# Two layers of a hybrid backbone on one core: the pieces of the stream work are moved between the engines' programs, and five mixed blocks go ahead of the heads

## The reference, cut to what matters

```
p = p + mu * (0.5 * (left neighbour + right neighbour) - p)
r, k, v, zw, za = split(p)
decay = exp(-exp(-softplus(-(w0 + tanh(zw) @ w2)) - 0.5))      # for each of two directions
a     = sigmoid(a0 + za @ a2)                                    # for each of two directions
kk    = k*k_k / max(norm(k*k_k), 1e-12)
kmod  = k * (1 + (a - 1) * k_a)
```

## Time and profile before

| what | us |
|---|---|
| median of three runs (2557.12 to 2574.31) | 2568.69 |
| the profiled execution's own time | 2581.38 |
| its span | 2579.6 |
| first load of the next stage (the scan) issued | 672.38 |

### The profile page before, as it was taken

The page is one execution under the profiler, slowest core; times in us unless marked ns, Lnnn a source line. Parts: engine busy times, 40 slices in busy tenths (PEclk is TensorE's granted clock), DMA queues, the critical chain, the costliest instruction groups (busy, mean ns, idle before and its releaser), DMA issues. The chain is left out here.

```text
span 2579.6 us, 61157 instructions
## 1 busy us (share of the span) xinstructions
PE 2130.2 (83%) x26174; PEld 1790.7 (69%) x26174; DVE 1292.5 (50%) x2064; ACT 871.7 (34%) x1685; POOL 722.2 (28%) x786
## 2 busy tenths in 40 slices
PE   3899998787367888878599996894999969999988
PEld 1667876565257777777488885673777758888866
DVE  4335467886334444444354443985546524444422
ACT  2223144465234434444133332222334302333311
POOL 2246322211123224233041000343357414100012
PEclk6999998898589999999799997896999979999989
DMA  8556444553322222220321104644344453111162
GB/s 296 180 145 161 131 143 152 180 182 127 112 80 80 64 81 70 61 86 24 87 82 42 42 27 138 189 140 162 105 110 110 112 140 99 58 50 51 39 201 90
DMA packets 228941, 285.70 MB, mean 111 GB/s; under 512 B 61529, under 2 KB 166905, under 8 KB 227649
## 3 DMA queue, kind: packets, MB, share of 16 engines
q1 hardware_dynamic: 190624, 176.52, 22.9%
q0 software_dynamic: 25680, 81.58, 9.9%
q10 hardware_dynamic: 12368, 23.70, 3.1%
HBM read 193.76 MB, written 87.95 MB: 109 GB/s over the span
## 5 line engine op out<-in xcount | busy, mean ns | idle before, releaser
L164 PE MATMUL in_acc<-in_hi,in_whi 128*128 128x512 f32 (+1 forms) x1024 | 400.6, 391 | 19.6 <-DVE in_lo L840 17.6
L164 PE MATMUL in_acc<-in_lo,in_whi 128*128 128x512 f32 (+1 forms) x1024 | 379.6, 371 | 0.0
L164 PE MATMUL in_acc<-in_hi,in_wlo 128*128 128x512 f32 (+1 forms) x1024 | 379.4, 371 | 0.0
L164 PEld LDWEIGHTS in_acc<-in_hi,in_whi 128*128 128x128 f32 x1024 | 199.2, 195 | 72.3 <-issue 42.3
L164 PEld LDWEIGHTS in_acc<-in_lo,in_whi 128*128 128x128 f32 x1024 | 199.2, 195 | 35.2 <-issue 5.3
L164 PEld LDWEIGHTS in_acc<-in_hi,in_wlo 128*128 128x128 f32 x1024 | 198.5, 194 | 33.2
L1939 DVE TENSOR_REDUCE window_top<-window_score 128x1 f32<-128x640 f32 (+1 forms) x128 | 101.3, 791 | 185.2 <-PE window_score L2022 185.1
L1939 DVE TENSOR_REDUCE dense_top<-dense_score 128x1 f32<-128x640 f32 (+1 forms) x144 | 112.3, 780 | 162.0 <-PE dense_score L2026 161.8
L2064 PEld LDWEIGHTS dense_outs<-dense_V,dense_p 128*128 128x128 f32 x1344 | 169.5, 191 | 8.5 <-ACT dense_p L1907 4.9
L2064 PE MATMUL dense_outs<-dense_V,dense_p 128*128 128x65 f32 x1344 | 169.9, 269 | 0.9 <-ACT dense_p L1907 0.8
L2064 PE MATMUL window_outs<-window_V,window_p 128*128 128x65 f32 x1216 | 160.8, 276 | 1.6 <-ACT window_p L1907 1.1
(11 more groups left out here) (268 smaller groups left out, 5161.6 us busy)
## 6 DMA issues: line engine op xcount, KB each, us to landing
streams<-in_streams_out POOLq DMA_DIRECT2D x40, 512.0 KB, 3.8
scan_L<-streams SPq DMA_DIRECT2D x80, 256.0 KB, 3.7
in_wl<-in_w_mod ACTq DMA_DIRECT2D x32, 512.0 KB, 4.5
in_raw<-in_w_in_even SPq DMA_DIRECT2D x28, 512.0 KB, 4.3
in_raw<-in_w_in_odd SPq DMA_DIRECT2D x20, 512.0 KB, 4.0
close_ga<-gates SPq DMA_DIRECT2D x18, 512.0 KB, 4.1
in_wm<-in_w_mod SPq DMA_DIRECT2D x8, 1024.0 KB, 12.3
gates<-in_outs POOLq DMA_DIRECT2D x32, 256.0 KB, 3.7
```

What stands on the lines that cost most here:

```text
L164: last = pe.matmul(out, a(k), b(k), start=(k == 0 and x == 0), stop=(k == n - 1 and x == 2))
```

## The change

All edits are in the first layer's `projected`; the jobs' order is given where it is called.

- The five mixed blocks zw, za, k0, r0 and v0 come first, then key, value and four query jobs (units 15 to 32), nine mixes (33 to 59), and all eight gates (60 to 83).
- Slots are spread evenly over iterations 38 to 87: 63 slots for 49 units. Two slots fall in iterations 41, 45, 49, 53, 57, 61, 64, 68, 72, 76, 80, 84 and 87. CLEAR_AT stays 36, slot 0 moves to iteration 38.
- PE runs its slots **before** `product(i)`. Its slot t has the first lora product of item t+2, the second of item t+1, `squares(t+1)` and the turned values of t-1. The second lora product and the squares have one buffer each.
- ACT's slot t has `exponentials(t-1)`, `rates(t+1)`, `root_keys(t-1)`, `square_keys(t+2)`, `values_out(t-2)`, in this order. DVE's has `unit_keys(t-2)` or `products(t-2)` with the bonus, then `clamp(t)` or `sums(t)`. POOL stores item t-3.
- The falling exponential is written shifted by one place into chunks of 65 with a 1 at the edge (`falls`, one buffer for each direction). One exponential of ACT and DVE's subtraction go; both products read `falls`. The first step of kmod moves from DVE (L979) to ACT.
- `load_z` has two loads less.

```diff
--- before.py
+++ after.py
...
-    CLEAR_AT, N_AT = 36, 40
+    CLEAR_AT, N_AT, FLUSH = 36, 38, 3
     slot_of_unit = [0] * (NU + 5)
     for u in range(NU + 5):
-        slot_of_unit[u] = min(len(items) + 1, max(0, min(u - N_AT, NSG) + max(0, (u - N_AT - NSG) * 27 // 20)))
+        slot_of_unit[u] = max(0, u - N_AT) * (len(items) + FLUSH) // (NU + 4 - N_AT)
...
-        return range(slot_of_unit[i], len(items) + 1 if i == NU + 3 else slot_of_unit[i + 1])
+        return range(slot_of_unit[i], slot_of_unit[i + 1])
...
-            ksq, root, norm = (st.sb(n, [P, 2, SG]) for n in ("ksq", "root", "norm"))
+            ksq, root, khalf, norm = (st.sb(n, [P, 2, SG]) for n in ("ksq", "root", "khalf", "norm"))
...
-            rate, sigs, cum, before = (st.sb(n, [P, 2, SG]) for n in ("rate", "sigs", "cum", "before"))
-            e_to, b_, bon = (st.sb(n, [P, SG]) for n in ("e_to", "b_", "bon"))
-            km = st.sb("km", [P, 2, SG])
+            rate, cum = (st.sb(n, [P, 2, SG]) for n in ("rate", "cum"))
+            sigs = st.sb("sigs", [P, 3, SG])
+            falls = st.sb("falls", [P, 2, SG // CHUNK, CHUNK + 1])
+            b_, bon = (st.sb(n, [P, SG]) for n in ("b_", "bon"))
+            km = st.sb("km", [P, 2, 2, SG])
...
-                    sp.wait_ge(cleared, 3)
+                    sp.wait_ge(cleared, 4)
                     sp.dma_start(tz[:], rkvz[12]).then_inc(z_in, 16)
-                    for d in range(2):
-                        sp.dma_start(za[(1 - d) * HD:(2 - d) * HD], rkvz[13][d * HD:(d + 1) * HD]).then_inc(z_in, 16)
-                        sp.dma_start(a2s[(1 - d) * HD:(2 - d) * HD], a2[d]).then_inc(dc_in, 16)
+                    sp.dma_start(za[:], rkvz[13]).then_inc(z_in, 16)
+                    sp.dma_start(a2s[:], a2.rearrange("d r n -> (d r) n")).then_inc(dc_in, 16)
...
+                        done = unit_of(items.index(("N", b - 1, NSG - 1)) + 2) + 1 if b else 0
...
+                            free = unit_of(items.index(("X", (q - 2) // NSG, (q - 2) % NSG, 1)) + 2) + 1 if q >= 2 else 0
...
-                        act.wait_ge(refined_k, q - 1)
...
-                    act.activation(ksq[:, q % 2], root[:, q % 2], ACT.Square, scale=0.5 ** 0.5).then_inc(halved_k, 1)
+                    act.activation(khalf[:, q % 2], root[:, q % 2], ACT.Square, scale=0.5 ** 0.5).then_inc(halved_k, 1)
...
-                        act.wait_ge(subtracted, n - 1)
+                        act.wait_ge(summed_r, n - 1)
...
-                    if n >= 2:
-                        act.wait_ge(mixed_k, n - 1)
-                    act.activation(sigs[:, h], aux[:, 2 + h, 0:SG], ACT.Tanh, scale=0.5, bias=a0h[:, d, b:b + 1]).then_inc(sig_done, 1)
+                    if n >= 3:
+                        act.wait_ge(b_made, n - 2)
+                    act.activation(sigs[:, n % 3], aux[:, 2, 0:SG], ACT.Tanh, scale=0.5, bias=a0h[:, d, b:b + 1]).then_inc(sig_done, 1)
+                    act.wait_ge(sig_done, n + 1)
+                    if q >= 2:
+                        act.wait_ge(bon_sum, q - 1)
+                    act.activation(km[:, q % 2, d], sigs[:, n % 3], ACT.Identity, scale=kac[:, b:b + 1], bias=kan[:, b:b + 1]).then_inc(mixed_k, 1)
...
-                    act.wait_ge(subtracted, n + 1)
-                    if n >= 1:
-                        act.wait_ge(r_done, n)
-                        act.wait_ge(totals, n)
-                    act.activation(e_to[:], cum[:, h], ACT.Exp, scale=-DECAY).then_inc(exp_to, 1)
-                    act.activation(before[:, h], before[:, h], ACT.Exp, scale=-DECAY).then_inc(exp_in, 1)
+                    act.wait_ge(summed_r, n + 1)
+                    if n >= 2:
+                        act.wait_ge(r_done, n - 1)
+                        act.wait_ge(a_done, n - 1)
+                        act.wait_ge(totals, n - 1)
+                    act.activation(falls[:, d, :, 1 - d:CHUNK + 1 - d], cum[:, h].rearrange("p (c n) -> p c n", n=CHUNK), ACT.Exp,
+                                   scale=-DECAY).then_inc(exp_to, 1)
                     act.wait_ge(exp_to, n + 1)
                     act.activation(cum[:, h], cum[:, h], ACT.Exp, scale=DECAY).then_inc(exp_from, 1)
...
                     act.activation(tot[:, d, :, s * PT:(s + 1) * PT].rearrange("p c t -> p t c"),
-                                   e_to[:, last::CHUNK].rearrange("p (t c) -> p t c", c=2), ACT.Copy).then_inc(totals, 1)
+                                   falls[:, d, :, CHUNK * (1 - d)].rearrange("p (t c) -> p t c", c=2), ACT.Copy).then_inc(totals, 1)
...
                 def slot(t):
                     if t == 0:
-                        act.wait_ge(z_in, 48)
-                        act.wait_ge(dc_in, 160)
+                        act.wait_ge(z_in, 32)
+                        act.wait_ge(dc_in, 144)
                         act.activation(tz[:], tz[:], ACT.Tanh).then_inc(tanhed, 1)
                         act.wait_ge(prepared, 5)
                         square_keys(0, 0)
-                    if item(t + 1)[0] == "N":
-                        square_keys(*item(t + 1)[1:])
+                        square_keys(0, 1)
                     if item(t - 1)[0] == "X":
                         exponentials(*item(t - 1)[1:])
-                        if item(t - 1)[3] == 1:
-                            values_out(*item(t - 1)[1:3])
-                    if item(t)[0] == "X":
-                        rates(*item(t)[1:])
-                    if item(t)[0] == "N":
-                        root_keys(*item(t)[1:])
+                    if item(t + 1)[0] == "X":
+                        rates(*item(t + 1)[1:])
+                    if item(t - 1)[0] == "N":
+                        root_keys(*item(t - 1)[1:])
+                    if item(t + 2)[0] == "N":
+                        square_keys(*item(t + 2)[1:])
+                    if item(t - 2)[0] == "X" and item(t - 2)[3] == 1:
+                        values_out(*item(t - 2)[1:3])
 
...
+                    pool.memset(falls[:], 1.0).then_inc(cleared, 1)
...
-                        if item(t - 1)[0] == "X":
-                            store_streams(*item(t - 1)[1:])
+                        if item(t - 3)[0] == "X":
+                            store_streams(*item(t - 3)[1:])
...
-                    dve.tensor_scalar(norm[:, q % 2], side[:, 0:SG], 1e-24, None, ALU.max).then_inc(clamped, 1)
+                    dve.tensor_scalar(norm[:, q % 2], aux[:, 3, 0:SG], 1e-24, None, ALU.max).then_inc(clamped, 1)
...
-                    dve.tensor_tensor(norm[:, h], norm[:, h], ksq[:, h], ALU.mult).then_inc(newton, 1)
+                    dve.tensor_tensor(norm[:, h], norm[:, h], khalf[:, h], ALU.mult).then_inc(newton, 1)
...
                         dve.wait_ge(b_done, n - 1)
                         dve.wait_ge(kd_done, n - 1)
-                        dve.wait_ge(a_done, n - 1)
                     dve.tensor_tensor_scan(cum[:, h, back], carry[:, d, back], rate[:, h, back], 0.0, ALU.mult, ALU.add).then_inc(summed_r, 1)
-                    dve.wait_ge(summed_r, n + 1)
-                    dve.tensor_tensor(before[:, h], cum[:, h], rate[:, h], ALU.subtract).then_inc(subtracted, 1)
...
-                        dve.wait_ge(kd_done, n)
-                    dve.scalar_tensor_tensor(b_[:], sigs[:, h], 1.0, kk[:, cols], ALU.add, ALU.mult).then_inc(b_made, 1)
-                    if d == 0 and q >= 1:
-                        dve.wait_ge(bon_sum, q)
-                    dve.tensor_scalar(km[:, d], sigs[:, h], kac[:, b:b + 1], kan[:, b:b + 1], ALU.mult, ALU.add).then_inc(mixed_k, 1)
+                    dve.scalar_tensor_tensor(b_[:], sigs[:, n % 3], 1.0, kk[:, cols], ALU.add, ALU.mult).then_inc(b_made, 1)
                     dve.wait_ge(mixed_k, n + 1)
                     dve.wait_ge(rkv_in[q % 2], (q // 2 + 1) * 16)
-                    dve.tensor_tensor(km[:, d], km[:, d], kept_[:, 1], ALU.mult).then_inc(km_done, 1)
+                    dve.tensor_tensor(km[:, q % 2, d], km[:, q % 2, d], kept_[:, 1], ALU.mult).then_inc(km_done, 1)
...
-                    dve.tensor_tensor(to[:, :, 0:P], by_tile(kept_[:, 0]), by_tile(e_to[:]), ALU.mult).then_inc(r_done, 1)
-                    dve.wait_ge(exp_in, n + 1)
-                    dve.tensor_tensor(to[:, :, P:2 * P], by_tile(kk[:, cols]), by_tile(before[:, h]), ALU.mult).then_inc(a_done, 1)
+                    dve.tensor_tensor(stream(0), by_chunk(kept_[:, 0]), falling(1 - d), ALU.mult).then_inc(r_done, 1)
+                    dve.tensor_tensor(stream(1), by_chunk(kk[:, cols]), falling(d), ALU.mult).then_inc(a_done, 1)
...
                 def slot(t):
                     if t == 0:
                         prepare()
+                    if item(t - 2)[0] == "N":
+                        unit_keys(*item(t - 2)[1:])
+                    if item(t - 2)[0] == "X":
+                        products(*item(t - 2)[1:])
+                        if item(t - 2)[3] == 1:
+                            bonus_of(*item(t - 2)[1:3])
```

(69 more changed lines are left out.)

23 lines of the change are left out of this document (13 added, 10 removed).

## The result

| what | before | after |
|---|---|---|
| median of four runs, us | 2570.48 (2557.12 to 2574.31) | 2608.97 (2604.02 to 2611.85) |
| the profiled execution, us | 2581.38 | 2609.64 |
| unit 36 begins | 302.53 | 298.67 |
| unit 38 begins | 313.44 | 319.58 |
| last product ends | 626.86 | 682.38 |

The ratio is 1.0156, with a 95% interval of 1.0126 to 1.0186: slower by 1.6%, where 1.2% was forecast. The medians are 38.5 us apart and the stage 39.1 us (672.38 to 711.50). The two profiled executions differ by 28.3 us only, because before's was 11 us above its median and after's was not; the 10.8 us that are missing lie in later stages, which the change does not touch. So I read the stage, not the span.

What follows compares the result with a forecast made beforehand. The prediction took a loop between DVE and ACT, not busy time, as the bound beside the streams. Streams' stretch +49 (109 instead of 60), tail -15.5 and front -2.7 gave +31, so 2599 us; range 2548 to 2632.

Steps and rivals of the forecast that it cites:

- lower bound of 81: Streams' stretch: added waits if splits ran as fast as alone and the clock never fell, instead of 109 us.
- idle time and slowed clock before, given back: Units 40 to 83 of the kernel before: 60 us, gone if nothing else waited once the DVE-ACT loop is cut.
- Item 1, the start: Iteration 38: PE waits before product 38 for loads, tanh, squares and clamp; 12 us, and 2 for the clock.
- Item 2, the N slots: Iterations such as 39, 51, 62 to 64, 74 to 76: single-buffered squares wait for DVE's clamp; 59 us.
- Item 3, the two-slot iterations: Iterations such as 45, 57, 72: the second slot's lora products wait for ACT's rate and tanh; 32 us.
- Item 4, the table loads: ACT in the streams' stretch: 28 table loads in place of 16, mostly hidden; PE sees 4 us.
- The tail: After PE's last product: with the DVE-ACT loop gone, DVE's remaining work takes 16 us; -15.5 us, at worst 0.
- The front: First head units, now 15 to 17 with filled queues instead of 6 to 8; -2.7 us, between 0 and -5.
- E: End of product i-1, when PE reaches its slot; whatever that needs from ACT's or DVE's iteration i is PE idle time.
- The clamps are ahead of PE: Rival, streams' stretch: DVE runs far ahead, only iteration 38, two-slot iterations and table loads cost; 2541 us, chance 0.2.
- The waits are half as long: Rival, waits for DVE's clamp: half of their 59 us gone, about equal at 2570 us; chance 0.3.
- The loop stays or the stores join it: Rival: DVE waits for each store's landing, tail gain lost, two-slot iterations two us more each; 2629 us, chance 0.08.

Runs made afterwards that it cites:

- Run 1: The changed kernel with the squares of the keys in two banks in turn, PE waiting for the clamp of one slot earlier; ratio 0.9969 to the kernel before.
- 11: The run 2 kernel with ACT also copying the turned values at the beginning of its slot; ratio 1.0084 to the kernel before.
- run 2: The changed kernel with the first lora product a slot later (item t+1) and two banks for the second; one run, 2635 us.
- 6: The changed kernel with the jobs in the old order of the kernel before; one run, 2620 us.
- 7: The kernel before with only the new order of the jobs; one run, 2586 us.
- Run 5: The changed kernel with PE's slots moved behind product(i), nothing else; ratio 0.9827 to the kernel before.
- run 8: The changed kernel with PE's slots behind product(i) and the squares in two banks; ratio 0.9779 to the kernel before.

## Why the prediction was right, point by point

The forecast was 2599 us, the result 2608.97; the stage grew by 39.1 us where 31 were forecast. The mechanism was right: PE's slots ahead of the product turned waits for ACT and DVE into idle time of PE. One term, the two-slot iterations, was half again too small, and part of the agreement of the others is luck, as said below. Two figures of the prediction don't follow from its own sum. The lower bound of 81 gives 81 - 60 - 15.5 - 2.7 = +3, so 2572 us and not 2580; and the last product would end at 626.9 - 2.7 + 49 = 673 and not near 670 (it ended at 682.4). The terms, in us above the kernel before:

| step | predicted | measured |
|---|---|---|
| front, before unit 36 | -2.7 | -3.9 |
| start, iteration 38 | 14 | 10.8 |
| N slots | 59 | 60.5 |
| two-slot iterations | 32 | 47.7 |
| table loads, as PE sees them | 4 | 0 to 1, and 2.6 within the N slots |
| idle time and slowed clock before, given back | -60 | -60 |
| tail | -15.5 | -16.4 |
| sum | +31 | +39.1 |

**Item 1, the start.** Right in kind: PE waits for ACT's first squared keys, 8.0 us in two brackets (7.38 and 0.62), where 10 to 14 of idle time were to be the sign. The loads landed earlier than I had them: ACT's last constants were there at 314.01, 15.3 us after unit 36 began, where I had 19.

**Item 2, the N slots.** Right in place and size. Iterations 39, 51, 62, 63 and 64 were predicted at 6.2, 9.4, 5.1, 8.2 and 7.7 us and measured at 6.7, 9.0, 6.4, 7.9 and 7.8; unit 50 at 1.4 and measured at none. Unit 64 agrees partly by luck: 1.28 us of its wait, and as much of that of unit 76, is a table load that the walk did not put there (item 4). Run 1 shows that the single bank is the cause: with two, these eight iterations, their slowed products counted, cost 47.4 us less, and the whole surplus is 43.8 lower. The rest is not given back because the squared keys come late next.

**Item 3, the two-slot iterations: the mis-sized term.** It was 32 and measured 47.7; the 15.7 between them are more than the whole miss of 8 us, and the start and the table loads, which came out smaller, gave back the rest. "Iterations with two slots among X items" counted only the lora products' wait for the rate and the tanh. What I left out stands behind these on ACT: the affine step of kmod, new on ACT with this change, waits for the bonus, and the copy of the values stands behind it, with PE's turned values waiting for the copy. Iterations 45, 57 and 72 were 5.4, 5.4 and 3.6 in the prediction and 9.0, 8.7 and 6.7 in the trace (less the pieces, and with the slowed product behind), 10.0 of the 15.7. Runs 2 and 11 show it: with the lora products' waits gone the three cost as much as before, with the copy in front they cost almost nothing. Iteration 49 (predicted 7.1, measured 8.1) and 61 (6.5 and 8.7) wait for the squared keys instead.

**Item 4, the table loads.** These are the groups of ACT from 298 to 705 us, busy and mean ns, then idle before:

```profile
L592 ACT ACT_TABLE_LOAD x14 | 18.0, 1283 | 0.3
...
L524 ACT ACT_TABLE_LOAD x8 | 10.3, 1283 | 40.6 <-PE in_acc L164 40.5
L602 ACT ACT_TABLE_LOAD x4 | 5.1, 1283 | 0.1
L622 ACT ACT_TABLE_LOAD x2 | 2.6, 1283 | 0.0
```

28 loads, as predicted, besides that of the first tanh. The place was wrong. At the changes from N to X PE sees next to nothing of them; but those of L524 stand ahead of the copy of the accumulator, and four of them begin only when a product has ended: they hold the 40.6 us of idle time. In iterations 64 and 76 PE waits for the end of the chain behind such a load. These are the timelines of ACT and DVE in iteration 64:

```profile
528.78 1.28 ACT L524 ACT_TABLE_LOAD   x1 [10.64 <-PE in_acc L164]
530.08 0.60 ACT L524 ACTIVATE in_xs<-in_acc 128x512 f32<-128x512 f32 x1
...
530.71 0.69 DVE L863 SCALAR_TENSOR_TENSOR in_outs<-in_xs,in_acc 128x512 f32<-128x512 f32 x1 [9.89 <-ACT in_xs L524]
```

Gate, unit keys and clamp (532.82) follow, and then the squares at 533.29. So 1.28 of the 4.59 us of idle time is the load, here and in iteration 76. The first tanh begins right behind its load, as before:

```profile
314.01 1.28 ACT L648 ACT_TABLE_LOAD   x1 [3.55 <-DMA in_a0h<-in_a_b]
315.30 1.27 ACT L648 ACTIVATE in_tz<-in_tz 128x1280 f32<-128x1280 f32 x1
```

The drain of 1.38 us that the Trainium skill ("ScalarE: Activation LUTs", What ACT_TABLE_LOAD costs) counts with each switch is not in this trace either: 0.01 us lie between load and tanh.

**The tail.** Right. The loop is cut: r products follow each other in DVE's timeline 2.0 to 3.5 us apart, where they were 5.6 apart in the earlier trace rows.

```profile
683.90 0.42 DVE L994 TENSOR_TENSOR in_streams_out<-in_rkv,in_falls 128x256 f32<-128x256 f32 x1
687.41 0.42 DVE L994 TENSOR_TENSOR in_streams_out<-in_rkv,in_falls 128x256 f32<-128x256 f32 x1
690.22 0.42 DVE L994 TENSOR_TENSOR in_streams_out<-in_rkv,in_falls 128x256 f32<-128x256 f32 x1
693.67 0.42 DVE L994 TENSOR_TENSOR in_streams_out<-in_rkv,in_falls 128x256 f32<-128x256 f32 x1
695.68 0.42 DVE L994 TENSOR_TENSOR in_streams_out<-in_rkv,in_falls 128x256 f32<-128x256 f32 x1
```

**The front.** The number agrees, the reason isn't shown: runs 6 and 7 leave it within the scatter.

**What the change was worth without its cost.** Run 5 has all of the change but PE's order, and its stage is 43.6 us shorter than before's: 25.3 of it are surplus (104.1 - 78.8), 13.9 the tail, the rest the front. So the shifted exponential, the moved pieces and the cut loop together gave the tail and 25 of the 60 us that were to go if nothing else waited, 41 of them with two banks for the squares (run 8); putting the slots ahead of the product cost 82.7 us. The prediction's core, that a product between E and the slot is what hides ACT and DVE, is what run 5 shows.

**The rivals.** "The clamps are ahead of PE" is out: eight waits of 3.8 to 7.3 us. "The waits are half as long" is out: 60.5 us where the forecast had 59. "The loop stays or the stores join it" is out: the tail gained its 16 us, and in units 38 to 83 DVE waits 5.2 us in all for streams to land.

**Open.** No run says how much of the gain of run 5 belongs to the shifted exponential alone, to the affine step on ACT, or to the slot distances; these were not tried one by one. Nor was the remedy of run 2 tried with the lora products still in opposite halves.
